# Moving the fine half of the normed rows by 32 bytes in SBUF

## The reference, cut to what matters

```python
x = x + 0.5 * _rmsnorm(_swiglu(_rmsnorm(x, ng[0]), w_ffn_up[layer, 0], w_ffn_down[layer, 0]), ng[1])
h = _rmsnorm(x, ng[2])
...
x = x + _rmsnorm(h, ng[3])
x = x + 0.5 * _rmsnorm(_swiglu(_rmsnorm(x, ng[4]), w_ffn_up[layer, 1], w_ffn_down[layer, 1]), ng[5])

def _swiglu(x, w_up, w_down):
    g, u = jnp.split(x @ w_up, 2, axis=-1)
    return (jax.nn.silu(g) * u) @ w_down
```

## The kernel before, in words

| tile | start before | past a multiple of 64 |
|---|---|---|
| raw, w_hi, w_lo | 16512, 49280, 65664 | 0 |
| xn_hi (g_xn0) | 91264 | 0 |
| xn_lo (g_xn1) | 100544 | 0 |
| y, sq, fbuf | 115008, 124224, 133440 | 0 |
| h_hi, h_lo | 138048, 163392 | 0 |
| a_cqh, a_cql | 182944, 186400 | 32 |
| second_hi, second_lo | 193344, 201536 | 0 |
| g_rowsr (line 1355) | 207008 | 32 |
| lead rows, six entries | 216224 | 32 |
| lead rows, entry behind the mLSTM layer | 213568 | 0 |
| a_rop, two buffers | 195232, 199328 | 32 |

## Time and profile before

### The profile page before, as it was taken

The page is one execution under the profiler, slowest core; times in us unless marked ns, Lnnn a source line. Parts: engine busy times, 40 slices in busy tenths (PEclk is TensorE's granted clock), DMA queues, the critical chain, the costliest instruction groups (busy, mean ns, idle before and its releaser), DMA issues.

```text
span 2529.1 us, 50748 instructions
## 1 busy us (share of the span) xinstructions
PE 2508.1 (99%) x21495; PEld 2411.4 (95%) x21495; DVE 1567.4 (62%) x1965; ACT 1185.0 (47%) x1622; POOL 304.9 (12%) x322
## 2 busy tenths in 40 slices
PE   9999999999999999999999999999999999999999
PEld 8999988999999987799999999999999999979999
DVE  5546967755665455575465556675566559767654
ACT  5434755543544355454354344454454447555443
POOL 1001015100200045010010000110010001052000
PEclk9999999999999999999999999999999999999999
DMA  7546624454554567454455465554455465335543
GB/s 224 166 138 177 179 79 152 158 166 138 180 166 142 179 185 210 136 166 159 148 177 166 139 186 183 159 184 162 146 175 166 142 189 168 94 114 177 166 141 111
DMA packets 425369, 404.23 MB, mean 160 GB/s; under 512 B 27996, under 2 KB 420824, under 8 KB 424888
## 3 DMA queue, kind: packets, MB, share of 16 engines
q1 hardware_dynamic: 420568, 392.44, 49.7%
q0 software_dynamic: 4480, 9.18, 1.2%
q10 hardware_dynamic: 144, 0.07, 0.0%
HBM read 385.25 MB, written 16.39 MB: 159 GB/s over the span
## 4 chain that ended last, share of the span: by engine, by line
PE 97%; DVE 1%; issue 1%; ACT 1%; DMA 0%; SPq 0%; DVEq 0%; ACTq 0%
PE psum L412 25%; PE psum L413 25%; PE psum L414 24%; PE psum L732 2%; PE psum L736 2%; PE psum L733 2%; PE psum L3247 1%; PE psum L1435 1%; PE psum L3260 1%; PE psum L514 1%; PE psum L1449 1%; PE psum L3286 1%; PE psum L1542 1%; PE psum L496 0%; PE psum L1579 0%
## 5 line engine op out<-in xcount | busy, mean ns | idle before, releaser
L392 DVE TENSOR_TENSOR w_lo<-raw,w_hi 128x2048 fp32r<-128x2048 f32 (+3 forms) x361 | 738.3, 2045 | 496.0 <-ACT w_hi L375 495.3
L412 PE MATMUL psum<-xn_hi,w_hi 128*128 128x288 f32 x3296 | 973.5, 295 | 0.9 <-issue 0.4
L413 PE MATMUL psum<-xn_lo,w_hi 128*128 128x288 f32 x3296 | 972.6, 295 | 0.0
L414 PE MATMUL psum<-xn_hi,w_lo 128*128 128x288 f32 x3296 | 969.2, 294 | 0.0
L375 ACT ACTIVATE w_hi<-raw 128x2048 fp32r<-128x2048 f32 (+2 forms) x349 | 597.2, 1711 | 770.9 <-PE psum L414 756.0
L412 PEld LDWEIGHTS psum<-xn_hi,w_hi 128*128 128x128 f32 x3296 | 620.7, 188 | 6.9 <-issue 4.4
L413 PEld LDWEIGHTS psum<-xn_lo,w_hi 128*128 128x128 f32 x3296 | 618.8, 188 | 0.7
L414 PEld LDWEIGHTS psum<-xn_hi,w_lo 128*128 128x128 f32 x3296 | 619.4, 188 | 0.0
L413 PE MATMUL psum<-h_lo,w_hi 128*128 128x288 f32 x1408 | 415.5, 295 | 0.0
L414 PE MATMUL psum<-h_hi,w_lo 128*128 128x288 f32 x1408 | 415.0, 295 | 0.0
L412 PE MATMUL psum<-h_hi,w_hi 128*128 128x288 f32 x1408 | 414.8, 295 | 0.0
(11 more groups left out here) (671 smaller groups left out, 2997.2 us busy)
## 6 DMA issues: line engine op xcount, KB each, us to landing
raw<-w_ffn_up SPq DMA_DIRECT2D x175, 1024.0 KB, 5.1
raw<-w_ffn_down SPq DMA_DIRECT2D x64, 768.0 KB, 4.3
raw<-w_ffn_down SPq DMA_DIRECT2D x64, 640.0 KB, 4.1
raw<-gdn_w_in SPq DMA_DIRECT2D x32, 1024.0 KB, 5.7
raw<-mlstm_w_in SPq DMA_DIRECT2D x12, 1024.0 KB, 5.3
raw<-gdn_w_out SPq DMA_DIRECT2D x8, 1024.0 KB, 6.0
raw<-cache_mla_latent SPq DMA_DIRECT2D x36, 128.0 KB, 3.6
a_split<-cache_mla_latent SPq DMA_DIRECT2D x36, 128.0 KB, 3.1
```

The costliest lines, as they stand in the source:

```text
L392: dve.tensor_tensor(spread(w_lo[slot(u, i)], u), packed(raw[u % NRAW], u), spread(w_hi[slot(u, i)], u).bitcast(F32), ALU.subtract).then_in ...
L412: pe.matmul(out, wh[:, k, c], hi(k), start=st, stop=False)
L413: pe.matmul(out, wh[:, k, c], lo(k), start=False, stop=False)
L414: last = pe.matmul(out, wl[:, k, c], hi(k), start=False, stop=sp_)
```

## The change

The unused tile between xn_hi and xn_lo shrinks from 16 to 8 words (64 to 32 bytes), the one behind xn_lo grows from 16 to 24 words (64 to 96 bytes). xn_lo, and g_xn1 with it, starts at byte 100512 instead of 100544. All other tiles and all instructions stay as they are, up to the address of that operand.

```diff
         xn_at = nc.sbuf_base
         xn_hi = sb("xn_hi", [P, KC, T], F32R)
-        between = sb("between", [P, 16])
+        between = sb("between", [P, 8])
         xlo_at = nc.sbuf_base
         xn_lo = sb("xn_lo", [P, KC, T], F32R)
-        behind = sb("behind", [P, 16])
+        behind = sb("behind", [P, 24])
```

## The result

The changed kernel takes 2541.11 us, the median of 5 runs (2538.23 to 2542.39); beside it the kernel before took 2531.20 us (5 runs, 2530.18 to 2531.93). The ratio is 1.0041, with a 95% interval of 1.0031 to 1.0052. So 32 bytes cost 9.9 us, 0.4%, which is clear of what a measurement can confuse with no change. It lies inside the range on record and on the side of rival 1, not of the forecast.

What follows compares the result with a forecast made beforehand. TensorE, busy 99% of the span at full clock, was taken as the bound. 0.5 ns x 3820 matmuls = +1.9 us, other users 0, on 2531.76 gave 2533.7 us; range 2526.5 to 2543.3 us.

Steps and rivals of the forecast that it cites:

- rival 1: Matmuls of lines 412 to 414: fine reads cost the whole triple, 1.3 to 3.0 ns each, +5.1 to +11.5 us; chance 0.17.
- The bound: Whole kernel: TensorE busy 99% of the span at full clock, lines 412 to 414 holding 74% of the chain.
- Every other user of the tile: VectorE's line 682, splits, state loads and GpSimd passes: costed at 0, between -0.5 and +0.5 us.
- The price: 3820 TensorE matmuls reading xn_lo: 0.5 ns more each when 32 past a multiple of 64, +1.9 us.
- dear end: Matmuls over xn_lo: a triple's whole loss hangs on the fine read, 3.0 ns each, +11.5 us.
- The control: Stream over a_cqh and a_cql, 32 past a multiple of 64: 132.6 ns a step, 0.4 more, taken as nearest in shape.
- So hi and lo in the same phase or in different ones makes no difference, as long as both are multiples of 64: TensorE streams: claimed from h_hi and h_lo at 132.3 ns a step against xn's 132.2.
- Rival 2: Matmuls over xn_lo: the shift loosens something, 1.4 ns less each, 5.3 us gained, 2526.5 us; chance 0.10.
- The rule on 16-byte lines: SBUF rows: crossing to a new line is penalised; a shift by 32 keeps the same 72 lines, so 0 us.
- rival 3: TensorE streams: no cost at all, control differences come from group size or bank changes, 2531.8 us; chance 0.31.

Runs made afterwards that it cites:

- e9: Changed kernel with the second and third matmul of each triple (lines 412 to 414) swapped, fine weight before fine row; 2532.81 us, ratio 1.0006.
- e6: Kernel before with 32 bytes ahead of xn_hi and none between, so both xn tiles sit 32 past a multiple of 128; 2551.74 us, ratio 1.0079.
- e8: Kernel before with h_hi, h_lo and everything behind moved by 64 bytes, h then level with the weights; 2536.01 us, ratio 1.0018.
- e2: Kernel before with no bytes between xn_hi and xn_lo, both then at 0 in a block of 128; 2541.37 us, ratio 1.0047.
- e1: Kernel before with 96 bytes between and 32 behind, xn_lo at byte 100576, 32 past a multiple of 64; 2531.13 us, ratio 1.0004.
- e3: Kernel before with xn_hi and xn_lo both 32 bytes higher, their distance kept; 2532.50 us, ratio 1.0010.
- e11: Kernel before with only coarse weights moved by 64 within 128 bytes, xn rows placed there as in the changed kernel; 2521.77 us, ratio 0.9964.
- e10: Kernel before with only fine weights moved by 64 bytes, xn rows placed within 128 bytes as in the changed kernel; 2535.40 us, ratio 1.0018.
- e7: Kernel before with both weights moved by 64 within 128 bytes, xn rows placed there as in the changed kernel; 2540.91 us, ratio 1.0042.
- e12: Kernel before with xn_hi moved to 64 and xn_lo to 96 in a block of 128, weights left at 0; 2537.52 us, ratio 1.0026.

## Why the prediction was right in its range and wrong in its forecast

**The bound** held: the time went into the TensorE streams over xn and nowhere else, at full clock, as the prediction said it would have to. Every other user of the tile was rightly costed at nothing (line 682, the state loads, the transfers).

**The price** is the step that failed: "3820 x 0.5 = 1.9 us", taken "from the longest such stream, since it has the same triple of lines". The long streams lost 3.3 ns a triple, between six and seven times 0.5 ns, and the result is 9.9 / 3820 = 2.6 ns for each matmul over xn_lo. It fell short of 3.3 because the entries lost only 0.4 ns a step instead of 1.1, the mLSTM's own loop (lines 2469 to 2471) 0.3, and TensorE's other work took 0.75 us less. Why the entries lost less is argued only. They too read the fine row behind the fine weight, as e9 does, but first go through the coarse row for all outputs, and about half of their weights are second_hi and second_lo, which start at 64 in a block of 128 and not at 0; no run tells the two apart.

That the range held is in part luck. Its dear end was 3.0 ns a triple, and the long streams went past it: 3820 x 3.3 would be 12.6 us, more than the 11.5 of the range.

**The control** was no control. I compared a_cqh and a_cql with xn by their place past a multiple of 64. Relative to the weights they are at 32 and 32, and the normed rows at that very place take 134.4 ns (e6), not 132.6. e8 shows that this stream answers to its place as well: at 96 and 96 it takes 133.3 ns, where xn has no run to compare with. Three rows to a group and weights 384 wide are a different sequence of reads, and e9 shows that the sequence alone can take the loss out of the long streams.

**"So hi and lo in the same phase or in different ones makes no difference, as long as both are multiples of 64"** is false. It was read from h at 64 and 64 and xn at 0 and 64, both of which happen to be fast. At 0 and 0, multiples of 64 too, both tiles have the loss (e2, e8).

**Rival 1** has the right sign and size, and the wrong mechanism: it blamed leaving a multiple of 64. e1 leaves it the same way and costs nothing, e3 moves all three off it and costs nothing in the stream. A chance of 0.17 for the right time rested on a wrong reason. Its steps, 132.7 to 133.2 ns, end just short of the 133.3 that came.

**Rival 2**, that a step could be under 132 ns by a better place, was not what this change did, but it is real: 131.1 over xn in e11 and 131.7 over h in e10. "None of the streams above comes under 132" was true, and was no evidence, since all had both weights at the same place.

**The rule on 16-byte lines** (the Trainium skill, "SBUF — State Buffer", section "Specifications (TRN2)") would give no change, and so would rival 3: the measurement decides against both. The places tried were all multiples of 32, so of 16, and they differ by up to 3.3 ns a step (131.1 in e11, 134.4 in e6).

What stays open is the rule itself. It is shown that the step depends on the places of rows and weights relative to each other (e7 and e12; h in e8 against xn in e2), and on the order of the reads (e9). That these two do not fix it alone, e6 and e9 show, with two paces each for one set of places and one order. Nor is it shown that 128 bytes is the block that counts: no run moved the rows by 128 bytes against the weights and left the rest alone, and odd and even rows, which lie 128 apart within 256, have different single steps (139.2 and 130.8 ns behind line 412 in the changed kernel). Why 64 and 96 cost two thirds of what 0 and 32 cost, and why moving the coarse weights alone wins, no theory here says. In e7, e10 and e11 some tiles that TensorE does not read in these streams moved as well (x by 64 or 128 bytes, the raw buffers in e7 and e11 by 64, all behind by 256); that this does nothing to the streams is argued from e12 = e7, not tried by itself.

## What to carry to other kernels

Where TensorE streams back to back with a new weight load for every matmul, the start addresses of rows, coarse weights and fine weights are a parameter: write down their places within 128 bytes relative to each other, and time a few, because 32 to 64 unused bytes ahead of one tile or another moved this kernel by +0.8% (e6) to -0.4% (e11). Look at more than one stream of each, since two streams with the same places need not have the same pace (e6, e9). A padding found to be good for one layout is good for that layout and that order of matmuls only; any tile inserted ahead of it shifts it. And a control from another stream of the same kernel must agree in the whole sequence of reads, not in the one property under suspicion.

## What the runs showed of the hardware that was not expected

- Steps of the same matmul (288 columns, a new weight load, clock 1.00) come in a few sharp values: 131.1, 132.2, 132.8, 133.0, 133.3 and 134.4 ns over xn, each held over whole streams, and 132.2, 133.0 and 133.3 in more than one kernel. Four of them, 131.1, 132.2, 133.3 and 134.4, lie 1.1 ns apart, some 6.7 ns for the six matmuls of two rows; as an estimate, that is 16 periods of a clock of 2.4 GHz. The other two do not fit this ladder, and why the steps come so is open.
- One set of places and one order can have two steady paces in one kernel: 133.3 and 134.4 ns in e6, 132.8 and 132.2 in e9.
- The loss of one operand's place shows on another operand's line: the fine rows moved, and the record that grew is that of line 412, over the coarse rows (295 to 299 ns).
- Moving the weights by 64 bytes slowed the streams over h, whose own place in a block of 128 and of 256 bytes had not changed, from 132.3 to 133.2 ns (e7).
- Swapping the second and third matmul of a triple is worth 1.1 ns a step in the long streams at one placement (133.3 to 132.2) and half of that in the first stream (133.3 to 132.8), with no change in what is read.
